# Bias of an output projection as a one-row product on TensorE, other mark groups for GpSimd, and an earlier adaLN load order, in a two-layer decoder trunk

## The reference

```python
c_act = silu(c)
for i in range(2):
    sh1, sc1, g1, sh2, sc2, g2 = split(c_act @ ada_w[i] + ada_b[i], 6)
    h = rmsnorm(x, norm_mix_g[i]) * (1 + sc1) + sh1
    m = conformer_conv(h) if i == 0 else stick_breaking_attention(h)
    x = x + g1 * m
    h = rmsnorm(x, norm_ffn_g[i]) * (1 + sc2) + sh2
    x = x + g2 * peer(h)
return rmsnorm(x, final_g)

# conformer_conv ends with
u = silu(layernorm(u, ln_g, ln_b))
return u @ w_out + b_out
# peer: per token 8 heads x 16 picks of 16384 experts
act = gelu(u_tab[expert] . h) * gate
y = sum(act * v_tab[expert])
```

## Time and profile before

| | |
|---|---|
| median of 3 runs | 2995.14 us (2995.13 to 2999.14) |
| profiled execution | 2995.64 us, of which the span of instructions is 2993.8 us |
| mean granted PE clock | 0.973 of full speed |
| busy share of the span | PE 93%, PEld 66%, DVE 77%, ACT 17%, POOL 59% |
| DMA | 957.27 MB, mean 320 GB/s over the span |

### The profile page before, as it was taken

One profiled execution on the slowest core, in us unless ns is written; L12 is line 12 of the kernel. 1 busy time (PEld: TensorE's weight loads), 2 busy tenths in 40 slices (PEclk: granted clock), 3 DMA queues, 4 the chain that ended last, 5 costly groups with the idle time before them and its releaser, 6 DMA issues.

```text
span 2993.8 us, 46968 instructions
## 1 busy us (share of the span) xinstructions
PE 2789.6 (93%) x14854; PEld 1973.5 (66%) x14854; DVE 2291.0 (77%) x4869; ACT 521.5 (17%) x1264; POOL 1761.8 (59%) x1701
## 2 busy tenths in 40 slices
PE   7998889999999999999899988879999999999996
PEld 5776777666666666666678857766666666555553
DVE  3999998888888866666872665988888887666677
ACT  2123216100000000000243162260000000000001
POOL 0030559677777767665620461677777777777774
PEclk8998998999999999999899999989999999999999
DMA  8645455899999999999953312339999999999997
GB/s 330 241 148 219 155 209 180 338 410 410 410 410 410 409 410 410 409 409 393 363 217 127 141 57 99 135 128 393 410 409 410 410 410 409 410 410 410 410 410 317
DMA packets 242817, 957.27 MB, mean 320 GB/s; under 512 B 26952, under 2 KB 27128, under 8 KB 225016
## 3 DMA queue, kind: packets, MB, share of 16 engines
q0 software_dynamic: 147456, 536.94, 45.4%
q1 hardware_dynamic: 95224, 418.64, 35.9%
HBM read 953.37 MB, written 2.10 MB: 319 GB/s over the span
## 4 chain that ended last, share of the span: by engine, by line
DMA 29%; issue 20%; PE 18%; POOL 12%; DVE 11%; ACT 2%; DVEq 1%; POOLq 1%; ACTq 0%
DMA v_rows<-in_pk_v,idx_now 19%; DMA u_rows<-in_pk_u,idx_now 9%; PE acc L799 8%; POOL v_rows L605 5%; POOL u_rows L599 4%; PE acc L791 4%; DVE mod_rows L1963 3%; DVE u_rows L1935 1%; PE acc L1152 1%; POOL idx_now L594 1%; PE out_e L1121 1%; POOL mod_rows L670 1%; PE mid L936 1%; POOL region L671 1%; PE mid L1121 1%
## 5 line engine op out<-in xcount | busy, mean ns | idle before, releaser
L1152 PE MATMUL acc<-h_t,weights 128*128 128x256 f32 x4096 | 934.7, 381 | 0.0
L1152 PEld LDWEIGHTS acc<-h_t,weights 128*128 128x128 f32 x4096 | 778.0, 191 | 207.7 <-issue 114.5
L605 POOL DMA_INDIRECT v_rows<-in_pk_v,idx_now x456 | 622.5, 1365 | 328.5 <-DVE mod_rows L1963 192.0
L1963 DVE SCALAR_TENSOR_TENSOR mod_rows<-v_rows,dots_acts,mod_rows 128x1024 f32<-128x1024 f32 x454 | 583.8, 1286 | 255.7 <-DMA v_rows<-in_pk_v,idx_now 247.1
L599 POOL DMA_INDIRECT u_rows<-in_pk_u,idx_now x512 | 643.5, 1257 | 198.0 <-issue 142.5
L1935 DVE SCALAR_TENSOR_TENSOR u_rows<-u_rows,h_rows 128x1024 f32<-128x1024 f32 x512 | 626.3, 1224 | 168.0 <-DMA u_rows<-in_pk_u,idx_now 161.9
L1169 PE MATMUL out_e<-weights,mod_rows 128*128 128x512 f32 x1024 | 469.9, 602 | 27.8 <-DVE mod_rows L2031 27.7
L1169 PEld LDWEIGHTS out_e<-weights,mod_rows 128*128 128x128 f32 x1024 | 190.9, 191 | 233.5 <-issue 200.6
L799 PE MATMUL acc<-h_t,weights 128*128 128x256 f32 x1024 | 238.6, 395 | 13.3 <-ACT h_t L1376 8.8
L1169 PE MATMUL out_e<-weights,c_pad_room 128*128 128x512 f32 x512 | 233.1, 599 | 11.7 <-DVE c_pad_room L2031 11.7
L799 PEld LDWEIGHTS acc<-h_t,weights 128*128 128x128 f32 x1024 | 201.8, 199 | 47.4 <-ACT h_t L1376 9.4
(11 more groups left out here) (272 smaller groups left out, 2800.5 us busy)
## 6 DMA issues: line engine op xcount, KB each, us to landing
weights<-in_u_t SPq DMA_DIRECT2D x256, 512.0 KB
weights<-in_v_t SPq DMA_DIRECT2D x256, 512.0 KB, 6.8
weights<-in_pk SPq DMA_DIRECT2D x32, 1024.0 KB, 4.8
v_rows<-in_ada SPq DMA_DIRECT2D x30, 1024.0 KB, 6.5
weights<-in_w_qkv SPq DMA_DIRECT2D x24, 1024.0 KB, 4.9
weights<-in_w_in SPq DMA_DIRECT2D x16, 1024.0 KB, 7.8
weights<-in_ada SPq DMA_DIRECT2D x8, 1024.0 KB, 4.9
weights<-in_w_out SPq DMA_DIRECT2D x8, 1024.0 KB, 4.8
```

The source lines that it names most:

```text
L605: nc.gpsimd.indirect_dma_start(v_rows[:, r % VR, :], None, a["pk_v"], bass.IndirectOffsetOnAxis(ap=idx_now[:, 1, par, r:r + 1], axis=0)).t ...
L1152: last = nc.tensor.matmul(acc[s][:, 0:HALF], weights[:, s, k * P:(k + 1) * P], h_t[:, k, :], start=k == 0, stop=k == KB - 1)
L1963: stt_op(out=y, in0=v_rows[:, r % VR, :], scalar=acts[:, bass.ds(b * BATCH + r, 1)], in1=y, op0=ALU.mult, op1=ALU.add).then_inc(v_used, 1)
```

## The change

It has four edits.

1. **Bias.** `by_token` takes an optional bias. For `conv_out` it begins each chunk's bank with one matmul of `ones_row` (1 x 128) by the chunk's 256 bias values, repeated for both token tiles (1 x 512), and the 16 matmuls accumulate on it. `b_out` is loaded as one row of 4 KB. `add_bias` and `bias_added` are gone.
2. **Late adaLN chunks.** `LATE` goes from 6 to 2 and `SPARES` from 6 to 10. Chunks 0 to 9 of the spares are loaded during query chunks 0 to 5 of the second half, after `SPARES_AT`; chunks 7, 8 and 9 go to places that the ranking of the first half has used, and SP waits for POOL's eighth look-up before each of them.
3. **POOL's groups.** They are 11, 19, 26, 31. In `both` the third is made after the first pair of row loads and the fourth after the second pair.
4. **Second-round marks.** In `four`, `hots` stands ahead of the wait for the block's gelu and of the gate product.

```diff
-LATE, SPARES = 6, 6
+LATE, SPARES = 2, 10
+SPARES_AT = ((0, 6), (1,), (2,), (3, 7), (4, 8), (5, 9), (), ())
...
+        AFTER_RANKS = (7, 8, 9)
...
-        EIGHTH = 8
-        ITERS = GROUPS // EIGHTH
+        POOL_AT = (11, 19, 26, 31)
+        ITERS = len(POOL_AT)
...
-                    sp.dma_start(b_out_rows, a["b_out"].partition_broadcast(P)).then_inc(b_out_in, 16)
+                    sp.dma_start(b_out_row, a["b_out"].rearrange("(o n) -> o n", o=1)).then_inc(b_out_in, 16)
...
+                for i in (SPARES_AT[at[3]] if at[:3] == ("pk", 0, 1) else ()):
+                    if i in AFTER_RANKS:
+
+                        sp.wait_ge(looked_up, PK[0, 0] + PH)
+                    sp.dma_start(spare_slots[i], a["ada1"][ADA_CHUNKS - LATE - SPARES + i, :, :]).then_inc(spare_in[i], 16)
...
-                steps(nc.gpsimd.tensor_tensor(bias_rows, b_out_rows, g1_row, ALU.mult))
-                for h in range(2):
-                    for t in (2 * h, 2 * h + 1):
-                        last = nc.gpsimd.tensor_tensor(x[:, t, :], x[:, t, :], bias_rows, ALU.add)
-                    last.then_inc(bias_added, 1)
...
-                    eighth_hots(l, 1)
-                    both(q, 0, 0, (q, 1), {1: lambda: eighth_hots(l, 2), 3: lambda: eighth_hots(l, 3)})
+                    pool_hots(l, 1)
+                    both(q, 0, 0, (q, 1), {0: lambda: pool_hots(l, 2), 1: lambda: pool_hots(l, 3)})
...
+                if bias is not None:
+
+                    nc.tensor.matmul(to[:, :].rearrange("p (t n) -> p t n", t=2), ones_row[0:1, :],
+                                     bias[0:1, i * NC:(i + 1) * NC].unsqueeze(1).to_broadcast([1, 2, NC]), start=True, stop=False)
...
+                            if g == 0 and n % 2 == 0 and not (first and n == 0):
+                                hots(b, n // 2)
                             dve.wait_ge(e_gelu_ready, b * PER_BATCH + (dense_no(l, g) + n + 1))
                             tt_op(e_now, e_now, gate, ALU.mult).then_inc(e_act_ready, 1)
                             if n == 0 and not uneven:
                                 weigh(q, b)
-                            if g == 0 and n % 2 == 0 and not (first and n == 0):
-                                hots(b, n // 2)
```

More of the change, by code:

```diff
@@ L258, in build @@
         ada_slots = [v_rows[:, i:i + 2, :].rearrange("p r n -> p (r n)") for i in range(0, VR, 2)]
-        spare_slots = [region[:, at:at + CHUNK] for at in (0, 2048, 4336, 6384, 12800, 14848)]
+        spare_slots = ([region[:, at:at + CHUNK] for at in (0, 2048, 4336, 6384, 12800, 14848)] + [mod_rows[:, D:D + CHUNK]] +
+                       [region[:, at:at + CHUNK] for at in (8432, 10480)] + [u_rows[:, 4:6, :].rearrange("p r n -> p (r n)")])
+        AFTER_RANKS = (7, 8, 9)
         now = ([weights[:, i, :] for i in range(2)] +
@@ L285, in build @@
         ln_rstd = region[:, 8432:8688]
-        b_out_rows, bias_rows = h_rows[:, 0, :], h_rows[:, 1, :]
+        b_out_row = region[0:1, 8704:9728]
         c_sq = region[:, 12800:14848].rearrange("p (k t) -> p k t", k=KB)
@@ L410, in build @@
         block = ctx.enter_context(nc.Block())
-        EIGHTH = 8
-        ITERS = GROUPS // EIGHTH
+        POOL_AT = (11, 19, 26, 31)
+        ITERS = len(POOL_AT)
         EARLY = 5
-        BY_POOL = EIGHTH - 2
         OWN = GROUPS - ITERS
+        OWN_GROUPS = [n for n in range(GROUPS) if n not in POOL_AT]
         SLOTS = len(e_acts)
@@ L426, in own_no @@
         def own_no(n):
-            return n // EIGHTH * (EIGHTH - 1) + n % EIGHTH - (n % EIGHTH > BY_POOL)
+            return n - sum(m < n for m in POOL_AT)
         def group_of(m):
-            return m // (EIGHTH - 1) * EIGHTH + m % (EIGHTH - 1) + (m % (EIGHTH - 1) >= BY_POOL)
+            return OWN_GROUPS[m]
         def by_pool(n):
-            return n % EIGHTH == BY_POOL
+            return n in POOL_AT
         def dense_no(l, g, i=0):
@@ L556, in _ @@
                     sp.dma_start(ada_bias[:, :], a["ada_b"][1, :].rearrange("(i n) -> i n", n=NC)).then_inc(bias_in, 16)
-                if at[:3] == ("pk", 0, 1) and at[3] < SPARES:
-                    sp.dma_start(spare_slots[at[3]], a["ada1"][ADA_CHUNKS - LATE - SPARES + at[3], :, :]).then_inc(spare_in[at[3]], 16)
+                for i in (SPARES_AT[at[3]] if at[:3] == ("pk", 0, 1) else ()):
+                    if i in AFTER_RANKS:
+                        sp.wait_ge(looked_up, PK[0, 0] + PH)
+                    sp.dma_start(spare_slots[i], a["ada1"][ADA_CHUNKS - LATE - SPARES + i, :, :]).then_inc(spare_in[i], 16)
                 if n + 1 == AHEAD_AT:
@@ L659, in both, with pool_hots @@
                         between[r]()
-            def eighth_hots(l, j):
-                n = j * EIGHTH + BY_POOL
+            def pool_hots(l, j):
+                n = POOL_AT[j]
                 if j:
-                    pool.wait_ge(gates_full, l * ROUNDS * GROUPS + CREDIT + n - EIGHTH + 1)
+                    pool.wait_ge(gates_full, l * ROUNDS * GROUPS + CREDIT + POOL_AT[j - 1] + 1)
                 else:
@@ L748, in _ @@
                         u_row(q, 0, 0, r)
-                    eighth_hots(l, 0)
+                    pool_hots(l, 0)
                     for r in (4, 5, 6, 7):
                         u_row(q, 0, 0, r)
-                    eighth_hots(l, 1)
-                    both(q, 0, 0, (q, 1), {1: lambda: eighth_hots(l, 2), 3: lambda: eighth_hots(l, 3)})
+                    pool_hots(l, 1)
+                    both(q, 0, 0, (q, 1), {0: lambda: pool_hots(l, 2), 1: lambda: pool_hots(l, 3)})
                     both(q, 1, 1, (q, 2))
@@ L785, in chunk_in, with by_token @@
                 return weights[:, n % 2, :], acc[m % 2]
-            def by_token(stage, l, h, i, lhs):
+            def by_token(stage, l, h, i, lhs, bias=None):
                 w, to = chunk_in(stage, l, h, i)
+                if bias is not None:
+                    nc.tensor.matmul(to[:, :].rearrange("p (t n) -> p t n", t=2), ones_row[0:1, :],
+                                     bias[0:1, i * NC:(i + 1) * NC].unsqueeze(1).to_broadcast([1, 2, NC]), start=True, stop=False)
                 for tt in range(2):
@@ L791, in by_token @@
                         last = nc.tensor.matmul(to[:, tt * NC:(tt + 1) * NC], lhs(k, tt), w[:, k * NC:(k + 1) * NC],
-                                                start=k == 0, stop=k == KB - 1)
+                                                start=k == 0 and bias is None, stop=k == KB - 1 and (bias is None or tt == 1))
                 last.then_inc(acc_full, 1)
@@ L919, in conv_out @@
                     pe.wait_ge(silu_ready, 2 * h + 1)
+                    if h == 0:
+                        pe.wait_ge(b_out_in, 16)
                 def lhs(k, tt):
@@ L924, in lhs @@
                     return c_ts[h][:, k, tt * P:(tt + 1) * P]
-                by_token("out", 0, h, i, lhs)
+                by_token("out", 0, h, i, lhs, b_out_row)
             def score(l, h, i, bank=None):
@@ L1128, in first_gates @@
                     if by_pool(n):
-                        pe.wait_ge(pool_hots_ready, l * ITERS + n // EIGHTH + 1)
+                        pe.wait_ge(pool_hots_ready, l * ITERS + POOL_AT.index(n) + 1)
                         ones, twos = pool_hot1, pool_hot2
```

7 lines of the change are left out of this document (removed).

## The result

The changed kernel takes 3004.62 us (median of ten executions, 3000.74 to 3006.83), the kernel before beside it 2997.45 us (2995.13 to 2999.14): over all executions a ratio of 1.0022, with a 95% interval from 1.0013 to 1.0031. By the medians it is slower by 7.2 us; I had forecast 7.7 us less (7.2 against the median), with a range that ended at 2994.5 us.

The account below looks back on a forecast made before the run. It took the expert stages as bound by DMA, their start by DVE (layer 0) and the gate-group chain. Terms +1.3 + 0 - 8.5 - 0.5 + 0 = -7.7 us on 2995.64 gave 2987.9 us, range 2981.5 to 2994.5.

Parts of the forecast that it names:

- Edit 3, layer 1: Layer 1's gate groups: waits for POOL's marks vanish, full DMA rate about 8.5 us earlier; bounds 6 (PE decides) and 10.5.
- A group takes POOL 10.5 us.: Layer 1, POOL's last set: started after group 26's gates at 1996, group 31 is marked at 2006.5.
- PE still has a u block (3.45 us) and a gate group (1.1 us) after group 31: Layer 1: PE then starts its v product near 2011.6 against 2018.41, 6.8 us earlier.
- DVE does not stand behind it.: Layer 1: DVE is not held by the wait for group 31, so its gate product comes 9.3 us earlier.
- Edit 3, layer 0: Layer 0's gate groups: DVE and POOL's loads gain 1.2 us, PE's v product loses about 1; net -0.5 us.
- Rival 2: Expert stages: the rate follows PE's v product, not DVE; layer 1 gives only 6, layer 0 costs 1; 2991.9 us, chance 0.24.
- Rival 4: First rounds: gate products come too late for PE behind 2.4 us of marks; at 0.5 us each +21 us, 3009; chance 0.04.
- Rival 3: Layer 0's gate groups: the clock stays at the lower level for four more groups, 4 us more; 2991.9 us, chance 0.06.
- Edit 1, +1.3 us: First half of layer 0: most of DVE's 8.4 us relief becomes waiting for PE; net +1.3 us, bounds -2.4 to +3.5.
- Rival 1: First half of layer 0: DVE's 8.4 us relief from the bias passes through; 2978.2 us, chance 0.08.
- Edit 2, 0 us: Late adaLN chunks of layer 0: PE done some 12 us earlier but nothing uses it; 0 us, from 0 to +2.
- edit 4, 0 us: First rounds: marks come 0.3 to 0.6 us earlier, but removed waits are worth nothing at 409 GB/s; bounds -2 and 0.

Follow-up runs that it names:

- e2_groups: The kernel before with only POOL's groups moved to 11, 19, 26 and 31; ratio 1.0021 to the kernel before.
- e5_spacing7: The changed kernel with POOL's groups at 10, 17, 24 and 31 instead of 11, 19, 26 and 31; ratio 0.9976 to the kernel before.
- e6_act: The changed kernel with the rows' gelu moved ahead of the gelu of block 7; 3003.61 us, ratio 1.0023 to the kernel before.
- e11_spacing866: The changed kernel with POOL's groups at 10, 18, 24 and 31; ratio 0.9979 to the kernel before.
- e4_order: The kernel before with only second-round marks put ahead of the wait for a block's gelu; ratio 1.0001 to the kernel before.
- e1_bias: The kernel before with only the bias product moved to TensorE and GpSimd's bias work gone; ratio 0.9998 to the kernel before.
- e8_dose: The changed kernel with POOL's groups at 11, 18, 25 and 31; ratio 1.0003 to the kernel before.

## Why the prediction was wrong, point by point

In the profiled execution the three differences of the table add to 12.1 us more, where I had 7.7 us less. Of these 19.8 us layer 1 has 9.9, layer 0 has 7.8 and the first mark 2.1.

**Edit 3, layer 1, "about 8.5 us earlier": the step that failed.** Measured from the first mark, the v product came 1.4 us later (e2_groups: 2.3 us later). Up to group 26 the working held to about 1 us. I had its gates at 1996, and they came at 2007.1, where layer 1's first mark was itself 9.9 us late. Then three steps failed, one after the other:
- "A group takes POOL 10.5 us." It took 13.9. I took the length of a set that ran among DVE's first-round marks for one that ends in DVE's dot products. That set had met one dot product, and the mark beside it already showed the price; the set after it met none and took 9.3 us. I had the rule on shared ports before me for edit 1 and did not use it for the set that edit 3 moves. POOL and DVE in the kernel before:

```profile
1985.37 1.62 POOL L670 TENSOR_SCALAR mod_rows<-iota_keys,mod_rows 128x128 f32<-128x128 f32 x1
...
1984.72 1.54 DVE L1935 SCALAR_TENSOR_TENSOR u_rows<-u_rows,h_rows 128x1024 f32<-128x1024 f32 x1
```

- "PE still has a u block (3.45 us) and a gate group (1.1 us) after group 31": 8.4 us instead of 4.55. Even without a wait it is 6.8 (e5_spacing7), since a group of the second round (1.15 us) and 0.94 us of waiting for DVE's gate product stand there too. In the changed kernel the lower clock adds 2.7 us, and the wait for the gate product falls away. PE waited 7.01 us and I had put 3 to 5; what an idle PE pays afterwards had no term at all.
- "DVE does not stand behind it." It does, by ACT: 3.37 us for the last gates, 4.82 for the rows' gelu. e6_act, without this second wait, was no faster beyond noise, with PE's v product still late.

Without the wait the forecast's mechanism gives what I called the bound where PE decides: 5.8 us in e5_spacing7, 6.9 in e11_spacing866, not 8.5.

**Edit 3, layer 0, "-0.5 us", bounds -2 and +1.5: +7.3 us.** "By the same working" was the fault. I never wrote out when group 26 is done here. PE's pace is 2.14 us a group, so the four groups after 26 give POOL about 8.6 us against 10.5 even by my own figure, and PE waited only 1.22 us for POOL before. There was little to win and all of the new wait to lose. This term alone is 7.3 of the 10.3 us by which the profiled span grew.

**The rivals.** Rival 2, that the rate follows PE's v product, named the right mechanism (e6_act) with a wrong price. It took group 31 for a smaller gain, when it was a loss. Rival 4, my only slower case, did not happen: e4_order is 1.0001, the first round of layer 0 runs at 409 GB/s in e5_spacing7. Rival 3, a clock that stays low in layer 0's groups, did not happen either: they are back at 1.15 us from 474.01, where they were from 472.90 before, with a first mark that is 3.4 us later.

**Edit 1, +1.3 us with bounds -2.4 to +3.5.** Right in the main: DVE's relief turns into waits for PE. Two steps of the working were off. The product costs 1.05 us, not 0.92, and a chunk of the first projection 7.1 us, not 6.9, so PE ends that projection at 221.56 instead of 220.2; and DVE waits at the residuals before it waits for the mean. The first mark comes some 2 us late by the profiles; e1_bias, 0.9998, allows -3.3 to +2.1 us. Rival 1, the relief that passes through, is excluded.

**Edit 2, 0 us, and edit 4, 0 us.** Both right: 0.9996 and 1.0001. PE is done with adaLN's products at 440.1 and idle for 8.86 us ahead of the first group. Its first two groups took 3.82 us, the next 1.15 and the one at 470.32 again 1.97; before, the first four took 1.42 to 1.97 us each. So the longer idle time did not keep the clock low for longer.

**The sum.** The lower bounds of the terms add to -16.9; my -14.9 leaves out edit 4's -2. A quarter of 0.58 is 0.145, where I wrote 0.12. Neither changes the forecast.

## What to carry to other kernels

When work that goes through a single buffer is spread over a sequence, write out for every piece when its input is free, how long it takes beside the work that runs at that moment, and when it is due; the last piece has no slack behind it, and here two groups' distance turned a gain of 7 us into a loss of 7. Take a duration from a row whose neighbours on the other engines are those of the new place, not from the nearest row in the program. And where an edit makes TensorE idle, add what it pays after the pause to the pause itself.

## What the runs showed of the hardware that I had not expected

POOL's mark of 0.6 us takes 2.56 us when DVE runs two dot products of 1.22 us back to back, with no gap for POOL between them, and 1.7 us when it runs one; beside DVE's wide marks, as long but with one operand in PSUM, it takes 0.57 to 0.67 us. In a pause of 6.25 us with PE idle the granted clock was 0.50 of full speed (from 530 to 535), and the next 1.98 + 5.53 us of matmuls took 1.10 + 3.72 where there was no pause, so 2.7 us more; after 3.85 us of waiting in e8_dose the u block took 4.24 us. A one-row matmul of 512 columns costs 1.05 us, no less than one with 128 rows at 0.92: here the rows were not what was paid for.
